# Every fourth of the first 92 gathered rows of table u: product on GpSimd, sum on ACT, in place of DVE

## What is computed

```python
def peer(h, w_q, sub_keys, u, v):
    ...
    cv, ci = lax.top_k(cand.reshape(b, l, PEER_HEADS, kk * kk), kk)
    ...
    def block(args):
        hx, ex, gx = args
        act = jax.nn.gelu(jnp.einsum('tkd,td->tk', u[ex], hx), approximate=False)
        return jnp.einsum('tk,tkd->td', gx * act, v[ex])
```

## Time and profile before

| | |
|---|---|
| median of 3 runs | 3267.69 us (3262.09 to 3269.25) |
| profiled execution | 3267.57 us |
| its span, first to last instruction | 3265.8 us |
| busy: PE, DVE, ACT, POOL | 76%, 74%, 41%, 30% of the span |
| mean granted TensorE clock | 0.859 |
| HBM traffic | 265 GB/s over the span |
| first gather of table u, last one | 1915.9 us, 2610.6 us |
| dot products on DVE | 256, 577.8 us |

### The profile page before, as it was taken

The page is one execution under the profiler, slowest core; times in us unless marked ns, Lnnn a source line. Parts: engine busy times, 40 slices in busy tenths (PEclk is TensorE's granted clock), DMA queues, the critical chain, the costliest instruction groups (busy, mean ns, idle before and its releaser), DMA issues.

```text
span 3265.8 us, 40596 instructions
## 1 busy us (share of the span) xinstructions
PE 2480.3 (76%) x15686; PEld 2181.0 (67%) x15686; DVE 2431.6 (74%) x3265; ACT 1328.5 (41%) x1853; POOL 980.4 (30%) x689
## 2 busy tenths in 40 slices
PE   7899999999999998999999850000022259998997
PEld 2588888988888887899997850000022148886886
DVE  6767666876667664644554799999999988896885
ACT  6555554544554454533334320000133175342333
POOL 0000000111111100000000012588888836675660
PEclk9899999999999999999999975555555569998999
DMA  8877776544444348776554357999999959997894
GB/s 328 307 286 265 260 267 223 177 168 149 142 154 162 136 148 313 297 268 229 199 196 171 120 213 247 346 422 422 422 421 422 422 179 329 374 354 263 308 371 137
DMA packets 148970, 866.74 MB, mean 265 GB/s; under 512 B 17825, under 2 KB 30129, under 8 KB 70561
## 3 DMA queue, kind: packets, MB, share of 16 engines
q1 hardware_dynamic: 67690, 447.29, 37.5%
q0 software_dynamic: 70992, 406.04, 32.3%
q10 hardware_dynamic: 10096, 10.82, 0.9%
HBM read 836.75 MB, written 27.33 MB: 265 GB/s over the span
## 4 chain that ended last, share of the span: by engine, by line
PE 64%; POOL 14%; DVE 9%; issue 6%; DMA 5%; ACT 3%; SPq 0%; DVEq 0%; ACTq 0%
PE bank L1622 31%; POOL u_ring L624 14%; PE bank L1977 10%; PE bank L1608 9%; PE bank L1645 4%; DMA v_got<-in_v_rest,expert 2%; DVE u_ring L1498 2%; PE bank L1960 2%; DMA raw<-in_tiles 1%; PE bank L1768 1%; PE bank L1769 1%; DVE w_lo L1024 1%; PE bank L1731 1%; PE bank L1732 1%; DMA v_raw<-in_v_dense 1%
## 5 line engine op out<-in xcount | busy, mean ns | idle before, releaser
L1024 DVE TENSOR_TENSOR w_lo<-raw,w_hi 128x1024 fp32r<-128x1024 f32 x674 | 826.3, 1246 | 625.5 <-ACT w_hi L664 614.8
L664 ACT ACTIVATE w_hi<-raw 128x1024 fp32r<-128x1024 f32 x674 | 697.8, 1056 | 801.1 <-PE bank L1622 531.3
L624 POOL DMA_INDIRECT u_ring<-in_peer_u,expert x256 | 507.1, 1981 | 402.2 <-PE bank L1622 212.7
L1622 PE MATMUL bank<-h_lo,w_hi 128*128 128x256 f32 x2048 | 591.2, 289 | 18.4 <-DVE w_lo L1024 9.4
L1498 DVE CUSTOM_DVE_ANT_0 u_ring<-u_ring,h_t 128x2048 f32<-128x2048 f32 x256 | 577.8, 2284 | 17.1 <-DMA u_ring<-in_peer_u,expert 15.8
L1622 PE MATMUL bank<-h_hi,w_hi 128*128 128x256 f32 x2048 | 583.0, 285 | 0.0
L1622 PE MATMUL bank<-h_hi,w_lo 128*128 128x256 f32 x2048 | 582.8, 285 | 0.0
L1622 PEld LDWEIGHTS bank<-h_lo,w_hi 128*128 128x128 f32 x2048 | 395.2, 193 | 26.8 <-ACT gate_buf L891 7.6
L631 POOL DMA_INDIRECT v_got<-in_v_rest,expert x256 | 342.2, 1337 | 225.0 <-DVE peer_g L1527 178.6
L1622 PEld LDWEIGHTS bank<-h_hi,w_lo 128*128 128x128 f32 x2048 | 395.3, 193 | 1.9
L1622 PEld LDWEIGHTS bank<-h_hi,w_hi 128*128 128x128 f32 x2048 | 394.7, 193 | 0.0
(11 more groups left out here) (294 smaller groups left out, 4777.2 us busy)
## 6 DMA issues: line engine op xcount, KB each, us to landing
raw<-in_tiles SPq DMA_DIRECT2D x337, 1024.0 KB, 4.9
v_raw<-in_v_dense SPq DMA_DIRECT2D x128, 660.0 KB, 7.0
s_t<-in_states POOLq DMA_DIRECT2D x8, 512.0 KB, 5.4
y_hi_rows<-y_hi_e POOLq DMA_DIRECT2D x16, 256.0 KB, 4.5
y_lo_rows<-y_lo_e POOLq DMA_DIRECT2D x16, 256.0 KB, 4.6
gate_rows<-gate_buf ACTq DMA_DIRECT2D x8, 512.0 KB, 2.8
y_hi<-y_hi_rows POOLq DMA_DIRECT2D x1, 4096.0 KB, 26.8
y_lo<-y_lo_rows POOLq DMA_DIRECT2D x1, 4096.0 KB, 17.0
```

The source lines that it names most:

```text
L624: pool.indirect_dma_start(u_ring[s][:, e % U_RING], None, a["peer_u"][0], bass.IndirectOffsetOnAxis(ap=expert[:, s, k:k + 1], axis=0)).the ...
L664: act.activation(w_hi[:, n % RING], raw[:, slot % SLOTS, (n % 2) * 2 * CH:(n % 2 + 1) * 2 * CH], ACT.Copy) \
L1024: dve.tensor_tensor(w_lo[:, n % RING], raw[:, n // 2 % SLOTS, (n % 2) * 2 * CH:(n % 2 + 1) * 2 * CH], w_hi[:, n % RING].bitcast(F32), ALU. ...
L1622: ins = pe.matmul(spot if x.shape[1] == KT else spot.rearrange("p (s t) -> p s t", s=NS), w[:, col], moving, start=start and k == 0 and m ...
```

## The change

Rows 3, 7, ..., 91 of block 0 (`ON_POOL`, 23 of them) are no longer treated by DVE. GpSimd multiplies such a row by the activation in place (`times`); ACT then copies the product onto itself with a sum into `act_p` (`dot_sum`). In POOL's stream the multiply of row k - 5 stands right behind gather k. The wait of a gather for its slot looks at `u_summed`, if the row that leaves it is one of the 23, and otherwise at `u_used`, which now counts DVE's rows alone. `take` steps over the moved rows. The exponential for block 1 stands behind all 23 sums on ACT, and so `normalise(1)` stands behind `coefficients(0)` on DVE.

```diff
--- before.py
+++ after.py
@@ -105,6 +105,14 @@
     LAST[(_kind, _j)] = _n
 ADA_ORDER = [0, 4, 1, 5, 2, 6, 3, 7] + list(range(8, 24))
 WINDOWS = GROUPS + 1
+ON_POOL = [k for k in range(92) if k % 4 == 3]
+
+
+def dve_dots(e):
+
+    return e - len([k for k in ON_POOL if k < e])
+
+
 
 
 def accumulators():
@@ -409,6 +417,8 @@
         x2_saved = sem("x2_saved")
         u_in = [sem(f"u_in{n}") for n in range(U_RING)]
         u_used = sem("u_used")
+        u_times = sem("u_times")
+        u_summed = sem("u_summed")
         gelu_done = sem("gelu_done")
         coef_ready = sem("coef_ready")
         pick_turn = sem("pick_turn")
@@ -620,9 +630,18 @@
             def gather_u(s, k):
                 e = s * SEL + k
                 if e >= U_RING:
-                    pool.wait_ge(u_used, e - U_RING + 1)
+                    if e - U_RING in ON_POOL:
+                        pool.wait_ge(u_summed, ON_POOL.index(e - U_RING) + 1)
+                    else:
+                        pool.wait_ge(u_used, dve_dots(e - U_RING + 1))
                 pool.indirect_dma_start(u_ring[s][:, e % U_RING], None, a["peer_u"][0], bass.IndirectOffsetOnAxis(
                     ap=expert[:, s, k:k + 1], axis=0)).then_inc(u_in[e % U_RING], 16)
+
+            def times(k):
+                pool.wait_ge(h2_copied, 4)
+                pool.wait_ge(u_in[k % U_RING], 16 * (k // U_RING) + 16)
+                u = u_ring[0][:, k % U_RING]
+                pool.tensor_tensor(u, u, h2_t[:, 0], ALU.mult).then_inc(u_times, 1)
 
             def gather_v(e):
                 s, k, n = e // SEL, e % SEL, e % V_RING
@@ -638,13 +657,15 @@
                 if k == 6:
                     pool.wait_ge(h2_turn, 4)
                 gather_u(0, k)
+                if k - 5 in ON_POOL:
+                    times(k - 5)
             pool.wait_ge(chosen, 4 * NS)
             pool.wait_ge(x2_saved, 16)
             for k in range(SEL):
                 gather_u(1, k)
             for e in range(2):
                 gather_v(e)
-            pool.wait_ge(u_used, NS * SEL)
+            pool.wait_ge(u_used, dve_dots(NS * SEL))
             for e in range(2, 4):
                 gather_v(e)
             pool.wait_ge(pick_turn, NS)
@@ -947,9 +968,19 @@
                 for s in range(NS):
                     ins = act.activation(h2_t[:, s, q * CH:(q + 1) * CH], psum[2 * (q % 2) + s][:], ACT.Copy)
                 ins.then_inc(h2_copied, 1)
-            for s in range(NS):
+            def gates_exp(s):
                 act.wait_ge(gate_max, 4 * s + 4)
                 act.activation(gate_t[:, s], gate_t[:, s], ACT.Exp).then_inc(gate_exp, 1)
+
+            def dot_sum(n):
+                act.wait_ge(u_times, n + 1)
+                u = u_ring[0][:, ON_POOL[n] % U_RING]
+                act.activation(u, u, ACT.Copy, accum_out=act_p[:, 0, ON_POOL[n]:ON_POOL[n] + 1]).then_inc(u_summed, 1)
+
+            gates_exp(0)
+            for n in range(len(ON_POOL)):
+                dot_sum(n)
+            gates_exp(1)
 
             def dense_hi(i):
                 act.wait_ge(v_full[i % TABLE], 16 * (i // TABLE) + 16)
@@ -983,7 +1014,8 @@
                 act.activation(hot_b[:, q % 2], hot_b[:, q % 2], ACT.Relu, scale=-1.0, bias=1.0).then_inc(key_ready, 1)
 
             for s in range(NS):
-                act.wait_ge(u_used, (s + 1) * SEL)
+                act.wait_ge(u_used, dve_dots((s + 1) * SEL))
+                act.wait_ge(u_summed, len(ON_POOL))
                 act.activation(act_p[:, s], act_p[:, s], ACT.Gelu).then_inc(gelu_done, 1)
                 act.wait_ge(pick_turn, s + 1)
                 act.activation(pick_t[:].rearrange("p a b -> p (a b)"), psum[6][:, 0:3 * P], ACT.Copy).then_inc(pick_ready, 1)
@@ -1542,15 +1574,18 @@
             taken = [0]
 
             def take():
+                if taken[0] in ON_POOL:
+                    taken[0] += 1
                 expert_act(taken[0])
                 taken[0] += 1
             for j in range(4):
                 choose(1, j, take)
             normalise(0)
+            for e in range(taken[0], SEL):
+                if e not in ON_POOL:
+                    expert_act(e)
+            coefficients(0)
             normalise(1)
-            for e in range(taken[0], SEL):
-                expert_act(e)
-            coefficients(0)
             for k in range(SEL):
                 expert_act(SEL + k)
                 if k >= 16 and (k - 16) % 3 == 0 and (k - 16) // 3 < BATCHES:
```

## The result

The changed kernel takes 3326.76 us (median of four runs, 3325.31 to 3330.6), the kernel before 3265.18 us beside it (3262.09 to 3269.25). The ratio is 1.0193, 95% interval 1.0177 to 1.0208: slower by 1.9%, 61.6 us. Forecast were +44.3 us and 3312, with a range of 3272 to 3345. The profiled execution has 3325.31 us, 57.7 more than that of before.

A forecast was written before the change was run, and what follows sets the result against it. DVE was taken to bound the choosing stretch and rows 144 to 255, full DMA engines the rows to 144. Choosing +30.5, moved exponential -0.9, rows 42 to 144 +14.7: +44.3 us, 3312 us, range 3272 to 3345.

The forecast's parts named there:

- Turns between DVE and GpSimd: Throughout the moved rows: a two-SBUF-input operation on DVE or GpSimd waits for the whole of the other's; multiply taken as 4.0 us.
- What a moved row can win: Choosing stretch: 32 calls of take reach row 42 instead of 32; ten more rows fetched at 2.48 us, 24.8 us at most.
- The choosing stretch: 1940.1 to 2075, DVE setting the pace: eleven multiplies at mean 2.77 us lengthen it by 30.5 us, less 0.9.
- the case of a gap shorter than 1.5 us: Choosing stretch, gaps 0.91 and 1.22 us between rows: row goes first, the one after is held 1.30 and 1.65 us.
- Rows 42 to 144: After the choosing: POOL's queue delays gathers, then transfers and DVE; 286.2 us where before 271.5, +14.7.
- two slow rounds of 15.05: From row 42, DVE living on the full ring: four gathers and a multiply each held, 15.05 us per four rows.
- The moved exponential and ACT's sums: Exponential and normalise(1) moved behind row 91: -0.9 us in the choosing stretch; ACT's sums cost nothing.
- POOL keeping ahead: Rival, rows 42 to 91: gathers slip into DVE's idle gaps and DVE limits; +9, 3277 us; chance 0.17.
- no blocking: Rival: multiplies do not block DVE's rows, the 30.5 fall away, ten rows stay won; 3242 us; chance 0.12.
- The longer multiply: Rival: each of 23 multiplies takes 4.7 us, 16 us more, 3328, or 3338 with free gathers held; chance 0.06.

The follow-up runs named there:

- the two kernels with sums: Changed kernel and kernel before, each with DVE's dot product replaced by a one-input sum over the row: 3252.86 and 3255.7 us.
- the control: Kernel before the change, with DVE's dot product replaced by a one-input sum over the row: 3255.7 us, ratio 0.9974.
- The fill: Changed kernel with GpSimd filling the landed row with a constant (writes 2048 columns, reads nothing) in place of multiplying: 3246.62 us, ratio 0.9944.
- the later multiplies alone: Changed kernel with only the twelve rows 47 to 91 moved: 3309.09 us, ratio 1.0157.
- the first three variants: Changed kernel with only rows 3 to 43 moved, only rows 47 to 91 moved, or 1024 of 2048 columns multiplied: 3279.29, 3309.09, 3292.09 us.
- the changed kernel with sums: Changed kernel, GpSimd's multiplies kept, with DVE's dot product replaced by a one-input sum over the row: 3252.86 us, ratio 0.9959.
- the half multiply: Changed kernel with GpSimd multiplying only the first 1024 of a moved row's 2048 columns: 3292.09 us, ratio 1.0073.

## Why the prediction was right, point by point

**Turns between DVE and GpSimd: right.** Held rows, held multiplies (5.75) and held gathers are in the trace. That DVE's second input is what matters was argued from the kernel before; the two kernels with sums bear it out, since one and the same multiply costs 68.0 us beside two-input rows, and with one-input rows leaves the time 8.2 us below the control's. Under the sums only small steps with two inputs were held. The fill shows that on GpSimd's side an operation that reads nothing leaves the rows alone; a GpSimd operation with one input was not run. A port as such is in no trace: what is shown is which operations wait for which.

**What a moved row can win, 24.8 us for ten: right.** Without the multiply 24.7 were measured from row 0, 22.9 between the medians of the runs.

**The choosing stretch: right in kind, +29.6 forecast (30.5 less 0.9), +44.6 measured.** Two terms were too small. The first is the length of the multiply: 4.0 taken, 4.50 measured, 11 x 0.5 = 5.5 us. The row that I started from, 1.90 us for 1024, had broadcast inputs; over 1024 columns of two full rows it is 2.35. The second is the case of a gap shorter than 1.5 us, for which I let the row go first and the multiply wait. The trace shows the reverse: the row begun at 2002.96, 0.52 us ahead of the multiply, was the one to wait, and was held 4.9 us, where I had 2.4 for this place. Three of the eleven multiplies fell on such a gap (rows begun at 1986.22, 2002.96 and 2021.70, held 4.8, 4.9 and 4.5 us). With a multiply of 4.5 my rule gives 1.8, 2.9 and 2.2 for them, so 7.3 of the other 9.5 us are theirs. Who waits in this case was the step that I had wrong.

**Rows 42 to 144: right, +14.7 forecast, +21.8 measured.** A round was put at 13.3 us with a multiply of 4.0, so 13.8 with 4.5, and the mean step is 13.8. That the two agree so well is partly luck, for I had two slow rounds of 15.05 first, and there is one of 16.4 and then a mean of 13.6. The twelve rounds end at 2279.9, 166.3 us behind the choosing, where I had 163.1; from there to row 144 it takes 127.0 us where I had 123.1. So 3.2 of the missing 7.1 us lie in the rounds and 3.9 behind them; the cause of the latter stays open. The step on which it hung, that POOL and not DVE is late, was tested by the later multiplies alone: +43.5 where DVE's turns alone would give 12 to 15.

**The moved exponential and ACT's sums: right.** I gave the sums nothing and the exponential -0.9 in the choosing stretch. The kernel without the multiply keeps both and gains the full 24.7.

**The rivals.** POOL keeping ahead (3277) falls with the later multiplies alone, no blocking (3242) with every held row. The longer multiply was the right direction: with 4.5 us my sum gives 44.3 + 11.5 = 55.8, and 61.6 were measured. The figure of the Trainium skill, "GPSIMD Engine Reference", section on performance versus the Vector engine, 4497 ns for an addition of this size, was exact here (the multiplies have a median of 4503), and I should have trusted a measurement of the same shape over half a shape with other operands.

## What to carry to other kernels

Before work goes to GpSimd to relieve VectorE, look at what VectorE does at that moment. Here VectorE's operations with two SBUF inputs and GpSimd's multiply of two SBUF inputs never ran side by side in these traces, and a multiply of 4.5 us was put in VectorE's way to spare it a row of 2.2. Beside one-input searches the same multiply was free. In the choosing stretch eleven rows moved without regard to this made the kernel 0.65% slower, and eight multiplies started by a signal at the head of a run of searches gained 0.5%.

An engine that issues transfers in order is slowed by each extra wait in its stream: GpSimd needed 13.8 us for four gathers and a multiply, of which the multiply itself is 4.5. Count the waits per transfer, not only its busy time.

## What the hardware showed that I had not expected

A multiply can hold a row that began before it. In the choosing stretch a row that started 0.52 us ahead of the multiply's record, while the gather in front of it was under way, waited for the whole multiply. Later, rows went first and the multiply was held by 1.2 us, as the multiply of 2191.61 (5.73 us, above) by this one:

```profile
2190.68 2.30 DVE L1530 CUSTOM_DVE_ANT_0 u_ring<-u_ring,h_t 128x2048 f32<-128x2048 f32 x1 [1.12 <-DMA u_ring<-in_peer_u,expert]
```

The lead decides. In the changed kernel, the first three variants and the changed kernel with sums, 39 operations of DVE with two inputs were under way when a multiply's record began. All 28 with a lead of 0.64 us or less waited for the whole multiply, and all 11 with a lead of 0.67 us or more went first and held it by 1.2 to 1.5 us. So the place is taken some 0.65 us ahead of the multiply's recorded start, an estimate from these two bounds. That it is made while the gather is still being written is a guess.

A gather is held by DVE's two-input dot product (1.9 to 2.9 us) and not by a one-input sum of the same length (0.95 us). The Trainium skill, "SBUF — State Buffer", section "Who interferes with whom", says that descriptor making is stalled by two-port modes and infers that a two-input operation leaves it alone. Here it does not, for gathers whose offsets lie in SBUF. Whether the reading of those offsets is the cause was not tried.

GpSimd's multiply is quicker when its inputs are broadcast: 1.90 us over 1024 columns in the kernel before, 2.35 us over 1024 columns of two full rows in the half multiply.
